# Split the merge weights once, in the projections, and load both parts from DRAM for the second and third token group

## The reference, cut to what matters

```
z = h @ w_in                                   # the projections
y_f = fourier_mix(u_f) @ w_proj_f              # three branches, 256 + 256 + 512 rows of weights
y_p = pool_mix(u_p) @ w_proj_p
y_m = (sigmoid(o) * hm) @ w_proj_m
y = (g_f * y_f + g_p * y_p + g_m * y_m) @ w_out
x = x + gate1 * rms_norm(y)
```

## Time and profile before

| | |
|---|---|
| time, median of 3 runs | 1832.66 us (1832.02 to 1836.2) |
| profiled execution: its time / its span | 1833.42 / 1831.6 us |
| granted PE clock, mean | 0.988 |
| PE busy | 1763.1 us, 96% |
| DVE / ACT / POOL busy | 797.2 / 619.8 / 406.6 us |
| projections, first to last unit | about 48 to 282 us |
| stage E, groups 0, 1, 2 | about 795 to 874, 874 to 952, 952 to 1031 us |

### The profile page before, as it was taken

One profiled execution on the slowest core, in us unless ns is written; L12 is line 12 of the kernel. 1 busy time (PEld: TensorE's weight loads), 2 busy tenths in 40 slices (PEclk: granted clock), 3 DMA queues, 4 the chain that ended last, 5 costly groups with the idle time before them and its releaser, 6 DMA issues.

```text
span 1831.6 us, 24582 instructions
## 1 busy us (share of the span) xinstructions
PE 1763.1 (96%) x9754; PEld 1634.9 (89%) x9754; DVE 797.2 (44%) x1256; ACT 619.8 (34%) x1064; POOL 406.6 (22%) x476
## 2 busy tenths in 40 slices
PE   7899999999999999989999899999999999999997
PEld 3799998979999999988888799999999999888885
DVE  4410002333334444446867874444444433354543
ACT  5321113233222222223656572222222223343432
POOL 0400001322122233333414353222222210000000
PEclk9999999999999999999999999999999999999998
DMA  8544445654355556687857232222222226657572
GB/s 322 230 168 142 169 158 184 207 203 137 124 178 183 177 191 202 201 233 237 267 172 236 100 111 73 72 73 72 72 72 72 73 73 197 206 180 230 176 237 73
DMA packets 175880, 296.84 MB, mean 162 GB/s; under 512 B 12201, under 2 KB 122348, under 8 KB 175770
## 3 DMA queue, kind: packets, MB, share of 16 engines
q1 hardware_dynamic: 131904, 163.80, 27.7%
q0 software_dynamic: 27536, 91.31, 15.2%
q10 hardware_dynamic: 16336, 40.29, 6.6%
HBM read 227.58 MB, written 67.82 MB: 161 GB/s over the span
## 4 chain that ended last, share of the span: by engine, by line
PE 82%; DVE 6%; ACT 3%; DMA 3%; POOL 2%; issue 2%; ACTq 0%; DVEq 0%; POOLq 0%
PE bank L544 25%; PE bank L546 25%; PE bank L545 25%; PE bank L756 1%; DVE w_lo L1710 1%; PE bank L1000 1%; PE bank L1003 1%; PE bank L1010 1%; PE bank L1018 1%; DMA zt<-z_scratch 1%; POOL ya L2460 1%; DMA z_scratch<-z_st 1%; DVE mg L2034 1%; DVE h_lo L2241 1%; PE bank L764 1%
## 5 line engine op out<-in xcount | busy, mean ns | idle before, releaser
L1710 DVE TENSOR_TENSOR w_lo<-raw,w_hi 128x1024 fp32r<-128x1024 f32 x218 | 280.8, 1290 | 391.6 <-ACT w_hi L1253 391.1
L544 PE MATMUL bank<-h_hi,w_hi 128*128 128x384 f32 x1080 | 376.9, 349 | 7.6 <-DVE h_lo L2241 4.9
L545 PE MATMUL bank<-h_lo,w_hi 128*128 128x384 f32 x1080 | 366.7, 340 | 0.0
L546 PE MATMUL bank<-h_hi,w_lo 128*128 128x384 f32 x1080 | 366.4, 339 | 0.0
L1253 ACT CAST w_hi<-raw 128x1024 fp32r<-128x1024 f32 x218 | 226.8, 1052 | 292.4 <-PE bank L546 162.7
L544 PEld LDWEIGHTS bank<-h_hi,w_hi 128*128 128x128 f32 x1080 | 204.7, 190 | 24.6 <-ACT z_st L1308 10.1
L545 PEld LDWEIGHTS bank<-h_lo,w_hi 128*128 128x128 f32 x1080 | 205.0, 190 | 0.1
L546 PEld LDWEIGHTS bank<-h_hi,w_lo 128*128 128x128 f32 x1080 | 204.6, 189 | 0.0
L546 PE MATMUL bank<-w_hi,f_lo 128*128 128x512 f32 x396 | 158.0, 399 | 0.0
L545 PE MATMUL bank<-w_lo,f_hi 128*128 128x512 f32 x396 | 156.0, 394 | 0.0
L544 PE MATMUL bank<-w_hi,f_hi 128*128 128x512 f32 x396 | 155.2, 392 | 0.0
(11 more groups left out here) (318 smaller groups left out, 3151.0 us busy)
## 6 DMA issues: line engine op xcount, KB each, us to landing
raw<-in_w_stream SPq DMA_DIRECT2D x208, 512.0 KB, 4.4
z_scratch<-z_st ACTq DMA_DIRECT2D x44, 576.0 KB, 3.1
raw<-in_w_ada SPq DMA_DIRECT2D x35, 512.0 KB, 5.6
mg<-z_scratch ACTq DMA_DIRECT2D x24, 576.0 KB, 7.0
f_raw<-f_scratch SPq DMA_DIRECT2D x66, 192.0 KB, 4.3
zt<-z_scratch POOLq DMA_DIRECT2D x27, 256.0 KB, 3.6
xp_scratch<-x_in POOLq DMA_DIRECT2D x9, 512.0 KB, 12.5
raw<-in_k_dft SPq DMA_DIRECT2D x9, 512.0 KB, 3.6
```

What stands on the lines that cost most here:

```text
L544: pe.matmul(out, a_hi, b_hi, start=start, stop=False)
L545: pe.matmul(out, a_hi, b_lo, start=False, stop=False)
L546: return pe.matmul(out, a_lo, b_hi, start=False, stop=stop)
L1710: dve.tensor_tensor(w_lo[:, slot], raw[:, slot], w_hi[:, slot].bitcast(F32), ALU.subtract).then_inc(s_wlo, 1)
```

## The change

The 16 units of stage E are also split once in the projections. SP loads a unit into `e_raw` (`e_load`), ACT makes `e_hi` (`e_high`), DVE makes `e_lo` (`e_low`), POOL stores both to DRAM. Group 0 of stage E works as before. For groups 1 and 2 (`split_before`, 32 units) SP, ACT and DVE do nothing. POOL loads both parts straight into the slots of `w_hi` and `w_lo` (`split_load`). PE waits for these landings. The three buffers are single and lie where `xr` lay. The loop in SP's projections is written out, and the first four units of stage `fi` can be loaded into `raw` early.

```
 def e_load(u):                                     # SP, at the end of each z1_turn step
     sp.wait_ge(s_elo, u) if u else sp.wait_ge(s_xt, 2 * NT)
     sp.dma_start(e_raw[:], ...)

+            def e_high(u):                         # ACT, at the end of each z unit
+                act.wait_ge(s_eld, 16 * (u + 2))
+                if u:
+                    act.wait_ge(s_est, 32 * (u + 1))
+                act.copy(e_hi[:], e_raw[:]).then_inc(s_ehi, 1)

             def project():                         # DVE
-                with dve.Fori(0, Z1_UNITS // 4 - 1) as i:
-                    for u in range(4):
-                        split(i * 12 + (ADA_FIRST + 3 * u + AHEAD), ADA_FIRST + 3 * u + AHEAD, i * 4 + (u + 1))
-                for u in range(Z1_UNITS - 4, Z1_UNITS - 1):
-                    split(ADA_FIRST + 3 * u + AHEAD, ADA_FIRST + 3 * u + AHEAD, u + 1)
+                for zi in range(Z1_UNITS):
+                    if zi < Z1_UNITS - 1:
+                        split(ADA_FIRST + 3 * zi + AHEAD, ADA_FIRST + 3 * zi + AHEAD, zi + 1)
+                    e_low(zi)
                 for n in range(U_G, U_G + AHEAD + 1):
                     split(n, n)

             for c in range(NT):                    # POOL
                 pool.dma_start(xp_dram[c], x_in[:, c]).then_inc(s_xps, 16)
+            for u in range(E_UNITS):
+                pool.wait_ge(s_ehi, u + 1)
+                pool.dma_start(eh_dram[u], e_hi[:]).then_inc(s_est, 16)
+                pool.wait_ge(s_elo, u + 1)
+                pool.dma_start(el_dram[u], e_lo[:]).then_inc(s_est, 16)
             pool.wait_ge(s_xps, 16 * NT)
+            pool.wait_ge(s_est, 32 * (E_UNITS + 1))

+            def split_load(n):                     # POOL, four units ahead
+                if split_before(n):
+                    unit_done(pool, n - SPL)
+                    u = (n - U_PRE) % E_UNITS
+                    pool.dma_start(w_hi[:, n % SPL], eh_dram[u]).then_inc(s_pre[n % SPL], 16)
+                    pool.dma_start(w_lo[:, n % SPL], el_dram[u]).then_inc(s_pre[n % SPL], 16)

             def e1(g):                             # POOL
                 for c in range(KT):
                     pool.wait_ge(s_ym, x + 1)
+                    split_load(U_E + g * E_UNITS + c + SPL)
                     ...
             def e2(g):
                 for m in range(3 * g, 3 * g + 3):
                     x_load(m)
+                for k in range(KT):
+                    split_load(U_E + g * E_UNITS + KT + k + SPL)

             # ACT and DVE, in e1 and e2
-                    split(n + AHEAD, n + AHEAD)
+                    if not split_before(n + AHEAD):
+                        split(n + AHEAD, n + AHEAD)
```

More of the change, by code:

```diff
@@ L93 @@
 U_END = U_FO + NG * FT
+U_PRE, PRE = U_E + E_UNITS, (NG - 1) * E_UNITS
+PRE_BASE = (64, 48, 16 * 6, 16 * NT)
 W_OUT = Z_COUNT + KT
@@ L262, in build @@
         x_in = sb(s2, "x_in", [P, NT, D])
-        xr = sb(s2, "xr", [P, 3, D])
+        s2x = ExitStack()
+        xr = sb(s2x, "xr", [P, 3, D])
+        s2x.close()
+        e_raw = sb(s2, "e_raw", [P, D])
+        e_hi = sb(s2, "e_hi", [P, D], F32R)
+        e_lo = sb(s2, "e_lo", [P, D], F32R)
         c_pad = sb(s2, "c_pad", [P, KT, ADA_M])
@@ L421, in build @@
         s_tmm, s_tact, s_tdve = sem("t_transposed"), sem("t_act"), sem("t_dve")
-        s_kvst = sem("kv_stored")
+        s_kvst = sem("kv_stored_or_split_weights3")
         s_fmm, s_fev, s_fd, s_fout, s_fst = (sem(n) for n in ("dft_multiplied", "dft_cosines_out", "dft_mirrored",
-                                                              "dft_ready", "dft_stored"))
+                                                              "dft_ready", "dft_stored_or_split_weights2"))
         s_red, s_redc, s_alt = sem("u_reduced"), sem("u_chain"), sem("alternating_sum_ready")
         s_cmm, s_mev = sem("mix_multiplied"), sem("mix_evacuated")
-        s_mst = [sem(f"mix_stored{i}") for i in range(2)]
+        s_mst = [sem(f"mix_stored_or_split_weights{i}") for i in range(2)]
         s_pmm, s_pa, s_pd, s_wp = sem("pooled"), sem("pool_act"), sem("pool_dve"), sem("w_pool_landed")
@@ L446, in build @@
         s_new = sem("new_state_stored")
+        s_eld, s_est = s_base, s_pos
+        s_ehi, s_elo = sem("e_weights_high"), sem("e_weights_low")
+        s_pre = (s_mst[0], s_mst[1], s_fst, s_kvst)
         s_mx = [sem(f"mx_landed{i}") for i in range(MX)]
@@ L528, in split_index, with split_before, raw_before @@
         def split_index(n):
-            return n - ADA_UNITS
+            return n - ADA_UNITS - (PRE if isinstance(n, int) and n >= U_FF else 0)
+        def split_before(n):
+            return U_PRE <= n < U_FF
+        def raw_before(n):
+            return n - RAW if n < U_PRE or n - RAW >= U_FF else n - RAW - PRE
         def h_full(eng, g, k, done):
@@ L658, in z1_turn, with e_load @@
                     load((n0 + 2) % RAW, w_ada[bass.ds(i * (2 * RAW) + (ADA_FIRST + 2 * u + 1), 1)])
+                    e_load(i * RAW + u)
+            def e_load(u):
+                if u:
+                    sp.wait_ge(s_elo, u)
+                else:
+                    sp.wait_ge(s_xt, 2 * NT)
+                if u < KT:
+                    sp.dma_start(e_raw[:], w_stream[Z_COUNT + u]).then_inc(s_eld, 16)
+                else:
+                    sp.dma_start(e_raw[:].rearrange("p (c n) -> p c n", c=KT),
+                                 w_stream[W_OUT:W_OUT + KT, :, ktile(u - KT)].rearrange("c p n -> p c n")).then_inc(s_eld, 16)
             z1_turn(0, True)
@@ L662, in _ @@
             sp.dma_start(cst_p[:], k_cst[:, CB["pool"].start:]).then_inc(s_const, 16)
-            with sp.Fori(1, Z1_UNITS // RAW) as i:
+            for i in range(1, Z1_UNITS // RAW):
                 z1_turn(i, False)
@@ L732, in unit_ready @@
             def unit_ready(n):
-                pe.wait_ge(s_wlo, split_index(n) + 1)
+                if isinstance(n, int) and split_before(n):
+                    pe.wait_ge(s_pre[n % SPL], PRE_BASE[n % SPL] + 32 * ((n - U_PRE) // SPL + 1))
+                else:
+                    pe.wait_ge(s_wlo, split_index(n) + 1)
             def W(slot, k):
@@ L1326, in project @@
                         ada_out(ADA_FIRST // ADA_G + zi // 2, z_number(zi, None) + 2)
+                    e_high(zi)
                 for n in range(U_G + 1, U_G + AHEAD + 1):
@@ L1737, in modulation_rest, with e_low @@
                 dve.wait_ge(s_mod, 2)
-            def project():
-                with dve.Fori(0, Z1_UNITS // 4 - 1) as i:
-                    for u in range(4):
-                        split(i * 12 + (ADA_FIRST + 3 * u + AHEAD), ADA_FIRST + 3 * u + AHEAD, i * 4 + (u + 1))
-                for u in range(Z1_UNITS - 4, Z1_UNITS - 1):
-                    split(ADA_FIRST + 3 * u + AHEAD, ADA_FIRST + 3 * u + AHEAD, u + 1)
+            def e_low(u):
+                dve.wait_ge(s_ehi, u + 1)
+                if u:
+                    dve.wait_ge(s_est, 32 * (u + 1))
+                dve.tensor_tensor(e_lo[:], e_raw[:], e_hi[:].bitcast(F32), ALU.subtract).then_inc(s_elo, 1)
+            def project():
+                for zi in range(Z1_UNITS):
+                    if zi < Z1_UNITS - 1:
+                        split(ADA_FIRST + 3 * zi + AHEAD, ADA_FIRST + 3 * zi + AHEAD, zi + 1)
+                    e_low(zi)
                 for n in range(U_G, U_G + AHEAD + 1):
```

16 lines of the change are left out of this document (11 added, 5 removed).

## The result

The changed kernel takes 1847.52 us (median of 5 runs, 1844.13 to 1851.78), the kernel before on the same chip 1833.58 us (5 runs, 1832.02 to 1836.2). The ratio is 1.008, with a 95% interval of 1.0064 to 1.0097. So it is slower by 0.8%, some 14 us, where 8 were forecast. The profiled execution took 1849.15 us, span 1847.4; before it was 1833.42 and 1831.6.

What follows compares the result with a forecast made beforehand. The prediction took PE, busy 96% of the span, to bound the kernel. Projections +14.6 and stage E -6.5 (-13.5 + 7) made +8 us on 1833.4, so about 1841 us, range 1829 to 1857.

Steps and rivals of the forecast that it cites:

- (a): Start of projections: first part stores land late behind `xp_scratch` stores, delaying `z3`'s raw load; PE waits 6 us.
- the 0.8 of `z4`: Projections: `z4`'s load lies behind another `e_load` and two constant loads taking 2.7 us; 0.8 us taken as late.
- (b): End of projections: DVE does `e_low(15)` before splitting `U_G`; PE waits 4.4 us.
- Clock: Projections: the waits at `z3` and `U_G` are long enough for PE's clock to fall, 2 x 1.7 = 3.4 us.
- The steady part at nothing: Middle projection units: slack of a low part shrinks from 6.3 to 1.7 us, so no cost.
- Stage E, what goes: Groups 1 and 2: waits for `w_lo` 5.2 and `mg` 4.5, clock 1.3 and 1.5, small gaps 1; 13.5 us gained.
- What comes: Stage E: 16.3 MB at 385 GB/s in group 1's `e1` and 14.7 in group 2's come late; 7 us of new waits.
- The two issues ahead of `ya`: Stage E: POOL's two more issues per unit delay `ya` by 1.1 us, beside PE's work on following units; no cost.
- (1): Rival: DMA nowhere late, first two stores land by some 87 us; -7.4 us, 1825; chance 0.08.
- (2): Rival: (a) costs half and stage E gives 9 to 10 us; about +1, 1834; chance 0.2.
- (3): Rival: stage E bound by DMA at 302 GB/s; stage E +10, total +25, 1857 us; chance 0.15.
- (4): Rival: every projection unit's 1.7 us slack gone through slower float32r stores; 12 units x 1 us, 1853; chance 0.1.

Runs made afterwards that it cites:

- Experiment 2: Changed kernel with POOL's nine `xp_scratch` stores spread out, one behind each pair of part stores: 1841.48 us, ratio 1.0043.
- Experiment 3: Changed kernel with SP's `e_load` placed behind the next unit's raw load instead of ahead of it: 1845.02 us, ratio 1.0059.
- experiment 6: Changed kernel with `U_G` split before the last `e_low`, `xp_scratch` stores spread out and `e_load` behind the next raw load: 1828.24 us, ratio 0.9973.
- Experiment 1: Changed kernel with DVE splitting `U_G` before it makes the last `e_lo`: 1840.88 us, ratio 1.0047.
- experiment 7: Changed kernel loading only 128 of 1024 columns of each low part in groups 1 and 2: 1839.65 us, ratio 1.0031.
- Experiment 4: Changed kernel's projections alone: parts made and stored, but stage E loads raw weights and splits them as before: 1853.84 us, ratio 1.0106.
- experiment 5: Changed kernel's stage E alone: two raw units loaded in place of the parts, nothing made or stored in the projections: 1826.07 us, ratio 0.9965.
- experiment 8: Changed kernel with `mx_b` loads moved to unit 7 of `e1`, `x1` stores and `xt` loads to units 1 and 4 of `e2`: 1840.7 us, ratio 1.0034.
- experiment 10: Changed kernel with the edits of experiment 6 and experiment 8, plus SP's two constant loads behind the raw load of unit `U_G` + 2: 1820.8 us, ratio 0.9933.

## Why the prediction was right, and where it was off

The sign, the mechanism and the two places of the loss were right. The size was 6 us short. By its steps:

**(a) The start, `z3`: right.** Booked were 6 us of wait from a chain of stores landing at 92, SP issuing at 95, `z3` there at 101. Measured: 93.0, 95.7, 103.1, and 6.11 us. PE's need for `z3` had itself moved from 97.4 to 99.4 by the wait at `z2`, which is why landing 2 us later made no longer wait. Experiments 2 and 3 cut the chain at two different links: in one the wait went, in the other it shrank to 1.74 us.

**`z2`: the term that was missing.** The sum took `z3` as the first unit that could be late. But `z2`'s raw load (issued at 70.13) stands on SP directly behind the second `e_load` (69.75) and runs beside nine stores, and ACT sees it only at 82.27:

```profile
69.75 0.33 SPq L687 DMA_DIRECT2D e_raw<-in_w_stream  x1
70.13 1.74 SPq L638 DMA_DIRECT2D raw<-in_w_stream  x1
...
82.27 1.04 ACT L1290 CAST w_hi<-raw 128x1024 fp32r<-128x1024 f32 x1 [13.80 <-DMA raw<-in_w_stream]
```

That made 3.5 us. The prediction counted "one more load" in the backlog as a delay for `z3`, not for the unit whose own load was in it. With the 0.8 of `z4` not appearing (a unit behind one that is late has slack again), this is most of the miss here: 14.6 booked with bounds of 9 and 18, 16.7 + 1.6 of clock behind `U_G` = 18.3 measured. Experiment 2 shows what the 0.8 was worth once `z3` is on time: 4.8, and with SP's order mended too 1.4 (experiment 6).

**(b) The end, `U_G`: right.** 4.4 us booked and 4.30 measured; the last start differs from its forecast by the lateness already gathered. Experiment 1 confirms it with its clock, as far as 4 us allow.

**Clock: right.** Two times 1.7 us were booked. I read some 2.2 us behind `z3` and 1.6 behind `U_G`. Behind the 3.5 us of `z2` the clock stayed at 1.00.

**The steady part at nothing: right, but narrowly.** No middle unit of the changed kernel shows a wait for its low part, and the units there lose some 0.3 us in all. But of the 1.7 us of slack nothing was left at three of them: once the low part is ready at 206.99 and PE takes it at 207.12, and it is 0.14 us again at 235.7 and 264.3. Experiment 2, with the same order on SP, already shows three waits of 0.5 to 0.7 us. With the raw load ahead of `e_load` (experiment 6) the slack is back at 4 to 6 us. So that this term cost nothing was in part luck.

**Stage E, what goes: right.** The 5.2 us on `w_lo` are gone, and 3.1 of the 4.5 booked for `mg`. **What comes: right in bytes and rate, and in place but for the order of the two.** One wait of 4.12 us at unit 7 of `e1` in group 1, behind the `x1` stores; 7 us were booked for all, and experiment 7 gives 7.9. The prediction called unit 4 the worst, and there PE waited only 0.3.

**The two issues ahead of `ya`: wrong.** The prediction saw that POOL's two more issues per unit make `ya` 1.1 us later, and took it to lie beside PE's work. At unit 7, the last of `e1`, it does not. POOL before, and POOL after:

```profile
916.30 1.26 POOL L2458 TENSOR_TENSOR ya<-mg 128x384 f32<-128x384 f32 x1 [3.58 <-DVE mg L2034]
```

```profile
936.14 0.57 POOL L2511 DMA_DIRECT2D w_hi<-e_high_scratch  x1 [3.31 <-DVE mg L2087]
936.71 0.55 POOL L2512 DMA_DIRECT2D w_lo<-e_low_scratch  x1
937.25 1.05 POOL L2526 TENSOR_TENSOR ya<-mg 128x384 f32<-128x384 f32 x1
```

ACT waits for this `ya`, and the copies out of PSUM for which PE waits come behind:

```profile
939.77 0.51 ACT L1517 CAST yy_hi<-ya 128x384 fp32r<-128x384 f32 x1 [6.38 <-POOL ya L2528]
940.19 2.89 ACT L1565 ACTIVATE hraw<-bank,mod,A 128x128 f32<-128x128 f32 x8
```

From the end of DVE's `mg` to ACT's `yy_hi` pass 3.9 us, where before it was 2.8. In group 2 it is 3.6 against 2.5, and PE's wait for `B_raw` grew by the same 1.1 us. So of the 3.4 us that were left as they are because they "hang on ACT's chain", the 1.8 of the transposes is not in the new trace, and the 1.6 of `hraw` and `B_raw` became 4.6. Experiment 4 has no such issues on POOL and has the waits of before:

```profile
PE bank L564 <- ACT B_raw L1565: 1.3, 1, 1.3
PE bank L564 <- ACT hraw L1565: 0.3, 1, 0.3
```

Experiments 5 and 7 have the issues and waits of 4.6 and 4.5 us, the latter with no DMA late. In experiment 8 the two issues of `mx_b` (1.5 us) also stand ahead of this `ya`: the 2.8 us become 5.1, and the wait for `hraw` 3.9. The delay of 1.1 us is enough for all that `B_raw` gained in the changed kernel and for 1.1 of the 1.9 us at `hraw`; the rest is not traced. No run put the issues behind the additions of `ya`.

The stage's net gain, forecast as 6.5, is 2.4 in the two profiled executions, 4.8 to 6.3 in experiment 4 and 7.7 in experiment 5. The timed runs carry more weight than one pair of profiles, and by them the forecast stands, to about 4 us.

**What lies outside.** Between `U_G` and stage E the changed kernel's profile shows 3.8 us more, of which 1.6 is the clock behind `U_G`. The rest is a lower granted clock from 411 us on, at places where PE's waits are the same in both traces; the change does nothing there. In the 30 us that begin 130 us behind `U_G`'s first matmul the clock is 0.94 here, but also in experiment 5, whose projections are those of the kernel before, and it is 1.00 in experiments 1 and 10, which hold the change. So it goes with the single execution, though what sets it is not shown. The medians differ by 13.9 where the profiles differ by 15.7, so some 2 us of the profiles' difference may be no cost of the change. In single profiles, terms under 3 us can't be told from this.

**The rate: right.** Booked were 385 GB/s, and the trace has 393 in just this stretch. The Trainium skill ("DMA: Bandwidth & Descriptors", Specifications) gives some 358 GB/s per core, half of what it gives for the memory that two cores share; by it the 16.3 MB would have taken 45 us, an estimate. Here one core runs alone, and the measurement decides.

**The rivals.** (1) asked that the first stores land by 87; they landed at 93. (2) asked that (a) cost half; it cost all and `z2` on top. (3) asked for 302 GB/s; it was 393. (4) had its cause half right, the slack was gone at three of the middle units, but it cost some 0.3 us and not 12; that float32r stores are slower than others is not shown. The measured time lies between the forecast and (3) and (4), for none of their reasons.

## What to carry to other kernels

Work that lies beside idle engines is free by its sum and can still cost all of its price by its order: here 25 MB and some 37 us of passes cost 1.3 us in one pair of profiles, and where instructions stood at three places in the queues of POOL, SP and DVE cost 15.4. So before such work goes in, walk every queue that it joins for the first two rounds and the last one, where a backlog stands or where a due time is close, and ask at each link what is queued behind it, beginning with the unit in flight when the backlog forms. And when a stage has its DMA engines full, move what is due latest (stores, next group's loads) out of it before judging the change: that was worth 6.8 us at not a byte less. Count the issues too: each DMA took 0.55 us of POOL, and two of them ahead of an addition that the rest waits for came out on PE at the last unit of each `e1`, where too little stood behind it to cover them.

## What the runs showed of the hardware

- A backlog on one queue reaches across buffers. The first 512 KB store behind nine others took 20.6 us from issue to landing, the median of the 16 being 4.8. With single buffers this backlog became a wait of 6.1 us on PE.
- The DMA engines carried 16.13 MB of mixed rows, half of the packets under 2 KB, at 393 GB/s for 41 us. In the earlier trace rows it was 302 GB/s at a share of 0.94, that is 321 per full share, and now it is 393 at 1.09, or 361: a gain of 12%. It came with the parts' long rows in the place of the gathered ones, but no run changed the length of the rows alone.
- Through POOL's queue the 512 KB stores of float32r tiles took 4.8 us (`e_hi`) and 7.7 us (`e_lo`, issued 1.2 us behind) and their loads 5.8 and 6.6 us at the median, next to 4.3 and 7.8 us for plain raw loads. The traffic beside them differed, so this compares no types.
- Issuing one of these transfers kept POOL for 0.53 to 0.57 us.
- A wait of 6.1 us was followed by 1.2 GHz (clock 0.50) with 12 matmuls in 3.5 us, against 21 at 2.4 GHz. On top of a wait of 4 to 6 us come 1.6 to 2.2 us for it.
